# Token-tile order at the end of w_ff2 and w_down and at the start of the next projection, and VectorE's order at w_out and at the post-norms

## The chip, the cores and the metric
The kernel runs on one core of a Trainium2 chip, in one launch. The metric is the device time of that core in microseconds (us). TensorE (PE) multiplies, VectorE (DVE) and ScalarE (ACT) compute element by element, GpSimd (POOL) does small statistics and softmax scalings, and SyncE (SP) issues the transfers of the weights.

## The reference, cut to what matters
Four transformer layers run over 256 tokens of width 1024, all in fp32: two of a first kind, then two of a second.

```python
# first kind, x2
h = modulate(rmsnorm(x, norm1_g[l]), shift1, scale1)
proj = h @ w_in[l]                      # 1024 x 7200, with the gates
merged = g_a*(o_mla @ w_o_mla[l]) + g_b*(o_sb @ w_o_sb[l]) + g_c*(o_mb @ w_o_moba[l])
x = x + gate1 * (merged @ w_out[l])
h = modulate(rmsnorm(x, norm2_g[l]), shift2, scale2)
x = x + gate2 * (square(relu(h @ w_ff1[l])) @ w_ff2[l])     # w_ff2: 4096 x 1024
# between the kinds: x = rmsnorm(x, final_norm_g)
# second kind, x2
mix = hybrid_mixer(rms_norm(x, attn_pre_norm[l]), ...)      # w_in_2, attention, w_out_2
x = x + rms_norm(mix, attn_post_norm[l])
u = conv_ffn(rms_norm(x, ffn_pre_norm[l]), ...)             # w_up, conv, silu, w_down: 2816 x 1024
x = x + rms_norm(u, ffn_post_norm[l])
```

## The kernel before, in words
The 256 tokens are two token tiles, t = 0 and 1, of 128 each. A product of two fp32 values is made of three fast matmuls: each operand is split in a high part (rounded) and a low part (what is left), and high*high, high*low and low*high are added in PSUM (`three`).

Weights come in pieces of 128 x 1024 values (512 KB; 464 or 474 KB for the projections). A unit is four pieces. SyncE loads the pieces in stream order into a ring of ten places (`RAW`); the load of a piece waits until PE has told that the piece ten places earlier is used (`piece_used`, in the order of the stream). ScalarE then writes the piece's high part (L1195) into a second ring of four places (`HIGH`), whose place is free when PE has used the piece four earlier; the first unit of each projection has its high parts in `spare` memory instead. VectorE then writes the low part over the piece (L1562, `split_quarter`). Each engine works through its instructions strictly in the order in which the program has them. That order is written out by hand: `highs(n)` on ScalarE, `split_unit`, `first_quarters(n)` on VectorE.

`linear_deep` computes w_ff2 (8 units) and w_down (5 units of 4 pieces and one of 2). A piece here is 128 rows by all 1024 columns, and four PSUM banks collect t=0 (two halves of columns, i = 0 and 1) and t=1 (i = 2 and 3). Within a unit PE goes piece by piece over all four banks; in the last unit it goes bank by bank. The left operand is the hidden layer, split by VectorE unit by unit into two buffers used in turn (`split_hidden`, L1586 and L1587), in `split_unit(lambda j: hidden(g) if j == 0 else None)`, that is right behind the unit's first piece.

At the end of w_ff2 VectorE multiplies each bank by the gate row and adds it to x (`gated`, L1810 and L1812). ScalarE squares each part of x (L1214), GpSimd makes the reciprocal root (`rstd_parts`, L604), VectorE scales the tile (`scale_tokens`, L1555), PE turns it (`flip_tile`, eight transposes, L670), and both ScalarE and VectorE copy the turned tile out, in high and low parts (`features_out`, `split_tokens`, L1592 to L1596). Only then can the next projection start on this tile. Between the kinds of layer there is one more norm (`final_norm`, L1819). At the post-norms of the second kind the squares are of the banks, `normed` writes bank * rstd * row to `wide` (L1994) and adds it to x (L1997), and the same steps follow. GpSimd clears two buffers (L637, L638) at the start of each layer of the second kind, right behind the last root.

The first unit of a projection (`tokens_as_ready`) runs all of t=0, with the flips of t=1 behind its first quarter, then all of t=1. The units behind it run quarter by quarter over both tiles (`tokens_by_quarters`), and free a piece with each quarter. In layers of the first kind steps of the modulation (`ada_step`, two VectorE instructions on a piece of w_ada) are laid beside the units: `IN_STEPS` says how many pieces of w_ada follow each unit.

At w_out of the first kind `linear_pair` computes the third branch, (t=0: two units), (t=1: two units), with `flip_tile(merged, 0)` before the last. VectorE multiplies each bank by its gate (L1938), adds it to `wide` (L1940), and splits two pieces of w_out before the first of these four banks and two behind it.

Of the kernel before, what the change touches and what calls it, by code (L numbers as in the profile page):

```python
# [113 lines left out]
def two_blocks(nc, x_in, c_in, positions, w_ada, b_ada, norm1_g, norm2_g, w_in, q_norm_g, w_uq,  # L114
# [5 lines left out]
    with ctx:  # L120
# [3 lines left out]
        def sem(name):  # L124
# [11 lines left out]
            ("gates", [P, T, 3 * D]),  # L136
            ("ring", [P, RAW, PIECE]))
        with contextlib.ExitStack() as first:
            featT, oT, kvm, pT, sm, gates, ring = [first.enter_context(nc.sbuf_tensor(n, shape, F32)) for n, shape in shared]
        featT_r, oT_r, kvm_r, pT_r, sm_r, gates_r, ring_r = [sb(n + "_r", shape, F32R) for n, shape in shared]  # L140
# [4 lines left out]
        big = sb("big", [P, 33 * S])  # L145
# [19 lines left out]

        proj = big[:, 0:T * ATT].rearrange("p (t n) -> p t n", t=T)
# [25 lines left out]
        spare_1 = slots(kvm_r, 0, PIECE) + slots(sm_r, PIECE) + slots(pT_r, 0)  # L192
        spare_2 = slots(gates_r, 0, PIECE) + slots(sm_r, PIECE) + slots(pT_r, 0)
# [81 lines left out]
        gates_ready = sem("gates_ready")  # L275
        conv_done = sem("conv_done")
# [94 lines left out]
        IN_STEPS = [4, 4] + [2] * 8  # L371
        IN_OUT = {1: 4, 2: 5, 4: 6, 6: 7, 8: 8, 10: 9}
# [3 lines left out]
        for l in range(LAYERS1):  # L376
# [34 lines left out]
            for u in range(8):  # L411
                split(w_ff2[l], (0, D), rows=(4 * u, 4 * u + 4), per=1)
        for l in range(LAYERS2):
# [18 lines left out]
            for k0 in range(0, CH, 4):  # L432
                split(w_down[l], (0, D), rows=(k0, min(k0 + 4, CH)), per=1)
# [81 lines left out]
        def _(sp):  # L515
# [48 lines left out]
            for t in range(T):  # L564
                sp.wait_ge(part_ready, LAST_PART - 2 * (T - 1 - t))
                sp.dma_start(out[0][t * P:(t + 1) * P, :], x[:, t, :]).then_inc(out_stored, 16)
            sp.wait_ge(out_stored, 16 * T)
# [7 lines left out]
        def _(pool):  # L575
# [47 lines left out]
            TWICE = ((0, 0), (0, 1), (1, 0), (0, 0), (0, 1), (1, 1), (1, 0), (1, 1))  # L623
# [10 lines left out]
            rstd_parts(TWICE)  # L634
            for l in range(LAYERS2):
# [5 lines left out]
                rstd_parts(TWICE if l + 1 < LAYERS2 else IN_TURN)  # L641
# [3 lines left out]
        def _(pe):  # L645
# [130 lines left out]

            def gate_quarters():
# [82 lines left out]
            def linear_deep(chunks):  # L860
# [4 lines left out]
                for c0 in range(0, chunks, 4):  # L865
                    get, _n = next_quarters()
                    seen.more(hid_split)
                    k = min(4, chunks - c0)

                    last_unit = c0 + k == chunks  # L870
                    steps = [(i, kk) for i in range(4) for kk in range(k)] if last_unit else \
                        [(i, kk) for kk in range(k) for i in range(4)]
                    for i, kk in steps:
                        t, cols = i // 2, slice(i % 2 * 512, i % 2 * 512 + 512)
                        w = get(kk)
                        h = [hid_parts[:, c0 // 4 % 2, part, kk, t * P:(t + 1) * P] for part in range(2)]
                        last = c0 + kk == chunks - 1
                        three(open_[i][:, :], h, (w[0][:, 0, cols], w[1][:, 0, cols]), c0 + kk == 0, last,
                              owner[i].full if last else None)
                        if i == 3:  # L880
                            owed.append((piece_used, 1))
# [132 lines left out]
            for l in range(LAYERS1):  # L1014
# [7 lines left out]
                else:  # L1022
                    flip_tile(scaled, 0)
                    tokens_as_ready(scaled)
                for u in range(11):
                    if u == 0:
# [42 lines left out]
                linear_deep(FF1 // P)  # L1069

            for l in range(LAYERS2):
                flip_tile(scaled, 0)
                tokens_as_ready(scaled)
                in_2_tile0.append(made[id(for_act)])

# [1118 lines left out]
```

## Time and profile before

| | us |
|---|---|
| median of 3 runs | 1845.45 |
| lowest, highest | 1840.52, 1845.65 |
| the profiled execution | 1851.16 |
| its span, first to last instruction | 1849.4 |
| PE busy | 1724.8 (93%) |
| VectorE busy | 1180.2 (64%) |
| ScalarE busy | 836.0 (45%) |

The profile is of one execution. The granted TensorE clock was 0.971 of full on average over the span. Busy PE time includes matmuls at half clock, so 93% is not 93% of what the engine can do. A row of the waits says which engine's instruction at which line sat idle, for whom, how long in total, how often, and the longest. A row of the timeline has start, duration, engine, line, operation, output and inputs, count, and in square brackets the idle time before it with what ended it.

### The profile page before, as it was taken

To read this page: it belongs to the slowest core of one execution; us is meant where nothing else is said; L and a number is where in the kernel's file an instruction comes from. 1 tells how busy PE (TensorE), PEld (TensorE's weight loads), DVE (VectorE), ACT (ScalarE), POOL (GpSimd) and SP (SyncE) were. 2 spreads that over 40 slices of the span, in tenths; PEclk is the share of its full clock that TensorE was granted. 3 is DMA by queue.
4 is the path that set the end of the run, shared out by engine and by line. 5 is a ranking of instruction groups with operands and counts; after the bars stand their busy time and mean duration, and the time that the engine had idled before them with its cause. 6 is when DMAs were issued, how large, how long until landed. Compare 5 with 4: busy or idle time off the path is not lost. (4 is left out here: it accounts for less than half of the span.)

```text
span 1849.4 us, 25477 instructions
## 1 busy us (share of the span) xinstructions
PE 1724.8 (93%) x9675; PEld 1439.2 (78%) x9675; DVE 1180.2 (64%) x2144; ACT 836.0 (45%) x1467; POOL 127.9 (7%) x272
## 2 busy tenths in 40 slices
PE   7899999889999999998899989997999899979998
PEld 7787675579987886764799868755998687659996
DVE  3877555665667875556545675644778656537785
ACT  2345363245534442651455353453554444635553
POOL 1000111000000000210000010131000100410000
PEclk9999999989999999999899989898999999989999
DMA  9677424447765984336355537504655466036652
GB/s 330 256 263 243 137 92 159 160 143 255 263 192 162 338 269 140 114 105 214 129 188 194 193 119 215 161 1 137 183 183 185 147 194 182 1 114 183 183 186 86
DMA packets 185626, 323.75 MB, mean 175 GB/s; under 512 B 13508, under 2 KB 101152, under 8 KB 185504
## 3 DMA queue, kind: packets, MB, share of 16 engines
q1 hardware_dynamic: 182912, 320.54, 53.8%
q10 hardware_dynamic: 2592, 1.57, 0.3%
q8 instruction: 77, 1.26, 0.3%
q14 instruction: 45, 0.37, 0.1%
HBM read 321.02 MB, written 1.05 MB: 174 GB/s over the span
## 5 line engine op out<-in xcount | busy, mean ns | idle before, releaser
L1562 DVE TENSOR_TENSOR ring_r<-ring,high 128x1024 fp32r<-128x1024 f32 (+3 forms) x422 | 500.0, 1198 | 325.4 <-ACT high L1195 317.9
L1195 ACT ACTIVATE high<-ring 128x1024 fp32r<-128x1024 f32 (+3 forms) x422 | 435.1, 1039 | 552.4 <-PE bank L661 428.0
L661 PE MATMUL bank<-featT_r,high 128*128 128x256 f32 x1216 | 349.9, 288 | 17.6 <-DVE oT_r L1594 14.2
L661 PE MATMUL bank<-oT_r,high 128*128 128x256 f32 x1216 | 347.7, 286 | 0.0
L661 PE MATMUL bank<-featT_r,ring_r 128*128 128x256 f32 x1216 | 347.6, 286 | 0.0
L661 PE MATMUL bank<-ring_r,featT_r 128*128 128x464 f32 (+3 forms) x736 | 282.6, 384 | 0.0
L661 PE MATMUL bank<-high,gates_r 128*128 128x512 f32 x864 | 268.0, 390 | 2.2 <-DVE ring_r L1562 1.2
L661 PE MATMUL bank<-high,featT_r 128*128 128x512 f32 (+3 forms) x648 | 252.1, 389 | 9.3 <-DVE oT_r L1594 7.4
L661 PEld LDWEIGHTS bank<-featT_r,high 128*128 128x128 f32 x1216 | 237.3, 195 | 19.9 <-issue 16.0
L661 PE MATMUL bank<-high,oT_r 128*128 128x512 f32 (+3 forms) x648 | 246.6, 381 | 0.0
L661 PEld LDWEIGHTS bank<-oT_r,high 128*128 128x128 f32 x1216 | 237.4, 195 | 0.5 <-issue 0.5
L661 PEld LDWEIGHTS bank<-featT_r,ring_r 128*128 128x128 f32 x1216 | 237.1, 195 | 0.0
L661 PEld LDWEIGHTS bank<-high,gates_r 128*128 128x128 f32 x864 | 162.2, 188 | 37.6 <-DVE ring_r L1562 2.3
L661 PE MATMUL bank<-ring_r,gates_r 128*128 128x512 f32 x432 | 168.2, 389 | 0.0
L661 PEld LDWEIGHTS bank<-ring_r,featT_r 128*128 128x128 f32 x736 | 141.1, 192 | 21.1 <-issue 1.0
L661 PEld LDWEIGHTS bank<-high,featT_r 128*128 128x128 f32 x648 | 122.4, 189 | 33.6 <-issue 11.8
L661 PEld LDWEIGHTS bank<-high,oT_r 128*128 128x128 f32 x648 | 122.4, 189 | 18.8
L1642 DVE SCALAR_TENSOR_TENSOR ada<-ring,tiny,ada 128x512 f32<-128x512 f32 x154 | 115.4, 749 | 8.3 <-DMA ring<-in_w_ada 3.3
L611 POOL TENSOR_TENSOR sm<-sm,rs 128x128 f32<-128x128 f32 (+1 forms) x160 | 76.5, 510 | 389.5 <-DVEq L1738 389.5
L1276 ACT ACTIVATE sm<-sm,mx 128x128 f32<-128x128 f32 (+1 forms) x160 | 70.8, 443 | 57.3 <-DVE mx L1720 57.3
L661 PEld LDWEIGHTS bank<-ring_r,gates_r 128*128 128x128 f32 x432 | 81.1, 188 | 16.6
L600 POOL TENSOR_SCALAR stat<-stat 128x1 f32<-128x1 f32 x26 | 10.0, 386 | 981.0 <-ACT sm L1214 980.6
(242 smaller groups left out, 2002.2 us busy)
## 6 DMA issues: line engine op xcount, KB each, us to landing
ring<-in_w_ff SPq DMA_DIRECT2D x128, 512.0 KB, 4.4
ring<-in_w_ada SPq DMA_DIRECT2D x96, 512.0 KB, 5.3
ring<-in_w_up SPq DMA_DIRECT2D x176, 256.0 KB, 3.1
ring<-in_w_in SPq DMA_DIRECT2D x64, 464.0 KB, 5.4
ring<-in_w_in SPq DMA_DIRECT2D x48, 512.0 KB, 5.1
ring<-in_w_in SPq DMA_DIRECT2D x48, 474.0 KB, 4.2
ring<-in_w_down SPq DMA_DIRECT2D x44, 512.0 KB, 3.5
ring<-in_w_out SPq DMA_DIRECT2D x24, 512.0 KB, 5.3
```

The source lines that it names most:

```text
L600: pool.tensor_scalar(stat[:, 4 + t:5 + t], stat[:, 2 * t:2 * t + 1], EPS, None, ALU.add).then_inc(pool_chain, 1)
L611: ins = pool.tensor_tensor(sm[:, n, a:z], sm[:, n, a:z], rs[:, n, t:t + 1].to_broadcast([P, z - a]), ALU.mult)
L661: ins = pe.matmul(o, a, b, start=start, stop=stop, skip_group_check=True)
L1195: act.activation(it["high"], it["raw"], ACT.Copy).then_inc(high_ready, 1)
L1276: ins = act.activation(sm[:, n, cols], sm[:, n, cols], ACT.Exp, scale=jobs[i]["scale"], bias=mx[:, n, t:t + 1], accum_out=rs[:, n, t:t + 1])
L1562: dve.tensor_tensor(it["low"], it["raw"], it["high"].bitcast(F32), ALU.subtract).then_inc(low_ready, 1)
L1642: link(dve.scalar_tensor_tensor(out=acc, in0=row, scalar=by, in1=acc, op0=ALU.mult, op1=ALU.add))
```

## The change
`linear_deep` takes a list of unit sizes ([4]*8 for w_ff2, [4, 4, 4, 2, 4, 4] for w_down). Its last two units run by token tile: t=0 of the last but one, t=0 of the last, t=1 of the last but one, t=1 of the last. The turning of t=0 for the next projection is put inside the last unit's t=1 part. The last unit's high parts lie in spare memory (the buffer `big`). The next projection's first two units run t=0 of both, then t=1 of both, with the flips of t=1 inside the second. The modulation pieces beside these units move three units on. At w_out VectorE splits one piece behind each of the two t=0 banks and copies out the features of t=0 ahead of the last bank. At the post-norms the banks are multiplied by the row before the root is there, and one instruction multiplies by the root and adds to x. The result leaves in four transfers instead of two.

```diff
-        IN_STEPS = [4, 4] + [2] * 8
-        IN_OUT = {1: 4, 2: 5, 4: 6, 6: 7, 8: 8, 10: 9}
+        IN_STEPS = [0, 4, 4, 4] + [2] * 6
+        IN_OUT = {2: 4, 3: 5, 4: 6, 6: 7, 8: 8, 10: 9}
+        FF_UNITS, DOWN_UNITS = [4] * 8, [4, 4, 4, 2, 4, 4]
...
+            def two_as_ready(second, flip_at):
+                units = [next_quarters() for _ in range(2)]
+                for t, u, r in ((0, 0, for_dve), (0, 1, outputs), (1, 0, for_dve), (1, 1, for_dve)):
+                    ...
+                    for j in range(QUARTERS):
+                        if t == 0 and u == 1 and j == flip_at:
+                            flip_tile(second, 1)
...
             def linear_deep(sizes, ready=None, flip_at=0):
+                for u in range(tail):
+                    ...
+                for t in range(T):
+                    if t == 0:
+                        seen.more(hid_split)
+                    for kk in range(sizes[tail]):
+                        for i in (2 * t, 2 * t + 1):
+                            step(tail, i, kk)
+                    if t == 0:
+                        seen.more(hid_split)
+                    for i in (2 * t, 2 * t + 1):
+                        if ready is not None and i == 2 + flip_at:
+                            flip_tile(ready, 0)
+                        for kk in range(sizes[tail + 1]):
+                            step(tail + 1, i, kk)
...
+                    first_quarters(2)
+                    gated(l - 1, 1, 0, for_dve, 0, 0)
+                    gated(l - 1, 1, 1, for_dve, 0, 1)
+                    first_quarters(1)
                     scale_tokens([0])
+                    first_quarters(1)
+                    features_out(gain, shift, True, [0])
+                    gated(l - 1, 1, 2, outputs, 1, 0)
                     gated(l - 1, 1, 3, outputs, 1, 1)
+                    first_quarters(2)
                     scale_tokens([1])
+                    first_quarters(2)
+                    in_out(for_dve, 0, 0)
                     features_out(gain, shift, True, [1])
...
-                        if br == 2 and k == 5:
-                            first_quarters(2)
+                        if br == 2 and not t:
+                            first_quarters(1)
+                        if br == 2 and t and not hf:
+                            features_out(parts=True, tiles=[0])
-                features_out(parts=True)
+                features_out(parts=True, tiles=[1])
...
-                    split_unit(lambda j: hidden(g) if j == 0 else None)
+                    split_unit(lambda j: hidden(g) if j == (3 if g == 7 else 0) else None)
...
+            def products(g, t):
+                    dve.wait_ge(squares, next(squared))
+                    ins = dve.tensor_tensor(wide[:, t, cols], b[:, :], rowbc[:, g, cols], ALU.mult)
+            def normed(t):
+                seen.more(rstd_ready)
+                    dve.scalar_tensor_tensor(out=x[:, t, cols], in0=wide[:, t, cols], scalar=stat[:, 8 + t:9 + t],
+                                             in1=x[:, t, cols], op0=ALU.mult, op1=ALU.add).then_inc(part_ready, 1)
...
-                for g in range(1, (CH + 3) // 4):
-                    split_unit(lambda j: hidden(g) if j == 0 else None)
+                for g in range(1, len(DOWN_UNITS)):
+                    at = {4: 2, 5: 3}.get(g, 0)
+                    split_unit(lambda j: hidden(g) if j == at else None)
```

## Rows read from the trace of the kernel before

**Rows 1.** PE's waits over the whole span, the three largest.
```profile
PE bank L661 <- DVE oT_r L1594: 31.8, 9, 4.8
PE bank L670 <- DVE wide L1555: 30.3, 8, 7.1
PE bank L661 <- DVE ring_r L1562: 11.9, 9, 4.8
```

**Rows 2.** Busy time by stretch (stretch, length, PE PEld DVE ACT POOL, clock, DMA share, GB/s).
```profile
554.20:603.80 49.60, 45.76 (x209) 38.66 (x208) 37.87 (x52) 20.40 (x32) 3.46 (x6) 0.97 0.55 175
1068.90:1125.20 56.30, 47.84 (x208) 39.52 (x208) 37.75 (x48) 24.43 (x42) 8.23 (x14) 0.91 0.50 154
1444.90:1500.80 55.90, 47.27 (x209) 39.80 (x208) 35.24 (x46) 24.33 (x42) 6.81 (x14) 0.91 0.51 154
336.10:352.10 16.00, 10.02 (x30) 6.66 (x31) 7.28 (x11) 1.61 (x3) 0.00 (x0) 0.79 0.43 133
1820.00:1849.40 29.40, 21.82 (x97) 17.73 (x95) 14.32 (x17) 8.06 (x13) 1.96 (x6) 0.96 0.09 36
```

**Rows 3.** PE alone by stretch: w_ff2-like matmuls, projection matmuls.
```profile
1792.56:1841.82 49.26, 49.26 (x216) 1.00 0.30 97
588.26:603.38 15.12, 15.12 (x74) 1.00 0.78 261
```

**Rows 4.** PE alone by stretch, where the granted clock fell and did not.
```profile
338.40:341.80 3.40, 3.40 (x10) 0.50 0.50 146
580.80:584.10 3.30, 3.08 (x9) 0.50 0.37 141
1096.20:1106.30 10.10, 6.31 (x21) 0.50 0.17 50
704.30:727.00 22.70, 22.66 (x65) 1.00 0.54 171
```

**Rows 5.** Timeline of VectorE and PE at the first w_out.
```profile
334.55 2.36 DVE L1562 TENSOR_TENSOR ring_r<-ring,high 128x1024 fp32r<-128x1024 f32 x2
336.82 0.68 DVE L1938 TENSOR_TENSOR big<-bank,gates 128x512 f32<-128x512 f32 x1
344.67 0.69 DVE L1938 TENSOR_TENSOR big<-bank,gates 128x512 f32<-128x512 f32 x1 [4.87 <-PE bank L661]
338.39 1.94 PE L670 MATMUL bank<-cst,wide 128*128 128x128 f32 x8 [2.30 <-issue]
348.25 0.47 PE L661 MATMUL bank<-high,featT_r 128*128 128x512 f32 x1 [3.69 <-DVE oT_r L1594]
```

**Rows 6.** Timeline of ScalarE and VectorE in the last units of w_ff2.
```profile
1079.79 1.06 ACT L1195 ACTIVATE high<-ring 128x1024 fp32r<-128x1024 f32 x1 [1.66 <-PE bank L661]
1080.88 1.23 DVE L1562 TENSOR_TENSOR ring_r<-ring,high 128x1024 fp32r<-128x1024 f32 x1 [1.49 <-ACT high L1195]
1073.87 0.69 DVE L1586 CAST gates_r<-big 128x1024 fp32r<-128x1024 f32 x1
1074.59 1.22 DVE L1587 TENSOR_TENSOR gates_r<-big,gates_r 128x1024 fp32r<-128x1024 f32 x1
```

**Rows 7.** SyncE's weight loads issued from 571 to 579 us.
```profile
DMA to landing us min/median/max: 3.6/4.9/5.5
```

**Rows 8.** Timeline of VectorE around the root of t=0, behind w_ff2.
```profile
573.59 0.69 DVE L1812 TENSOR_TENSOR x<-x,wide 128x512 f32<-128x512 f32 x1
576.34 0.75 DVE L1555 TENSOR_SCALAR wide<-x,stat 128x1024 f32<-128x1024 f32 x1 [0.73 <-POOL stat L604]
```

**Rows 9.** The scaling's and GpSimd's clearing's lines (duration ns min/median/max, first and last start).
```profile
L1555 DVE TENSOR_SCALAR wide<-x,stat x16: 745/753/2409, 10.4 to 1647.8; 128x1024 f32<-128x1024 f32 x16
L638 POOL MEMSET kvm<- x2: 1799/1799/1799, 1100.8 to 1476.2; 128x2048 f32 x2
```

**Rows 10.** Timeline of VectorE at a post-norm, t=1 behind w_out_2.
```profile
1267.43 0.75 DVE L1994 SCALAR_TENSOR_TENSOR wide<-bank,stat,rowbc 128x512 f32<-128x512 f32 x1 [1.86 <-POOL stat L604]
1268.21 0.69 DVE L1997 TENSOR_TENSOR x<-x,wide 128x512 f32<-128x512 f32 x1
```

More of the change, by code:

```diff
@@ L411, in two_blocks @@
             for u in range(8):
-                split(w_ff2[l], (0, D), rows=(4 * u, 4 * u + 4), per=1)
+                split(w_ff2[l], (0, D), rows=(4 * u, 4 * u + 4), per=1, spare=spare_ff if u == 7 else None)
         for l in range(LAYERS2):
@@ L431, in two_blocks @@
                 split(w_up[l], (a0, a0 + 256), (b0, b0 + 256))
-            for k0 in range(0, CH, 4):
-                split(w_down[l], (0, D), rows=(k0, min(k0 + 4, CH)), per=1)
+            for u, k0 in enumerate(itertools.accumulate(DOWN_UNITS[:-1], initial=0)):
+                split(w_down[l], (0, D), rows=(k0, k0 + DOWN_UNITS[u]), per=1,
+                      spare=spare_down if u == len(DOWN_UNITS) - 1 else None)
         MLA_FILL, MOBA_FILL = {1: 4, 4: 4}, {1: 2, 3: 4}
@@ L563, in _ @@
                     broadcast_rows(attn_post[l], ffn_post[l])
[L564 to L567, printed above, removed]
+            for n in range(2 * T):
+                t, cols = n // 2, slice(n % 2 * 512, n % 2 * 512 + 512)
+                sp.wait_ge(part_ready, LAST_PART - (2 * T - 1 - n))
+                sp.dma_start(out[0][t * P:(t + 1) * P, cols], x[:, t, cols]).then_inc(out_stored, 16)
+            sp.wait_ge(out_stored, 16 * 2 * T)
         N_LATE = 16 * (8 * DEPTH + 2)
@@ L864, in linear_deep @@
                 open_ = [claim(r)[0] for r in owner]
-                for c0 in range(0, chunks, 4):
-                    get, _n = next_quarters()
-                    seen.more(hid_split)
[L868 to L881, printed above, removed]
+                gets = [next_quarters()[0] for _ in sizes]
@@ new lines, in linear_deep, with step @@
+                first = list(itertools.accumulate(sizes, initial=0))
+                chunks, tail = first[-1], len(sizes) - 2
+                def step(u, i, kk):
+                    t, cols = i // 2, slice(i % 2 * 512, i % 2 * 512 + 512)
+                    w = gets[u](kk)
+                    h = [hid_parts[:, u % 2, part, kk, t * P:(t + 1) * P] for part in range(2)]
+                    c = first[u] + kk
+                    three(open_[i][:, :], h, (w[0][:, 0, cols], w[1][:, 0, cols]), c == 0, c == chunks - 1,
+                          owner[i].full if c == chunks - 1 else None)
+                    if i == 3:
+                        owed.append((piece_used, 1))
@@ L1083, in blocks_turned @@
                                  outputs.full if a and t else None)
[L1085 removed]
+                for u in range(2, 6):
                     tokens_by_quarters((for_act, for_dve), blocks_turned if u == 4 else None)
@@ L1160, in _ @@
                     channels(for_dve, True)
-                linear_deep(CH)
+                linear_deep(DOWN_UNITS, scaled if l + 1 < LAYERS2 else None, 1)
         @block.scalar
@@ L2005, in stored_units @@
                     stored(for_dve)
-                    dve.wait_ge(for_act.read, in_2_tile0[l] + n - 1)
-                for u in range(6):
+                    dve.wait_ge(for_act.read, in_2_tile0[l] + n - 2)
+                in_2_out(outputs, 0, 1)
+                split_unit()
+                in_2_out(for_dve, 1, 0)
+                in_2_out(for_dve, 1, 1)
+                for u in range(2, 6):
                     if u == 4:
```

164 lines of the change are left out of this document (106 added, 58 removed).

## The prediction
> **What bounds the kernel now.** I read the waits of PE first, because PE is busy in nearly the whole span. Only three kinds are large: for the low features (31.8 us, 9 times), for the scaled token tile (30.3 us, 8 times), for a split weight piece (11.9 us) [rows 1]. The first two are the serial chain behind each linear layer: bank, gate or norm, squares, root, scale, flip, features. Then I cut the span into the stretches where the change works [rows 2]. There are seven: two w_out, two post-norms behind w_out_2, and the ends of w_ff2 and w_down: tail A (w_ff2 to the second w_in), tail B (w_ff2 to w_in_2), tail C (w_down to w_in_2), and the last w_down, behind which the kernel ends. The rows run from the start of the last eight pieces to the end of the projection's second unit: A 49.6, B 56.3, C 55.9 us; the last stretch to the end of the kernel is 29.4 us.
>
> The same matmuls without a wait: 216 in 49.26 us are 0.228 us each, so eight pieces (96 matmuls) take 21.9; projection matmuls are about 0.212 (15.12 us for 72 of them whole), two units 20.4, 20.8 with w_in_2's 474 columns [rows 3]. With two flips of 1.1 us an ideal tail is 44.4 (A) or 44.8. So A has only 5.2 us to give, B 11.5, C 11.1.
>
> Part of this is clock. Behind a wait of 2.30 us the granted clock was 0.50 for 3.4 us, behind one of 2.8 as well, behind a wait of 4.1 with another of 3.1 in it for 10.1; behind one of 1.6 it stayed 1.00 [rows 4]. Half clock is the 1.2 GHz level instead of 2.4: it costs half of what PE worked in the stretch, some 1.6 us for 3.4.
>
> **w_out (twice).** Now VectorE splits two pieces (2.36 us) between the first two banks, so the second product starts at 336.82, and PE's flip waits 2.30 us, to 338.39. After the change one piece lies there, 1.14 less: the flip starts near 337.25 behind a wait of 1.2 us. That is below the waits behind which the clock fell, so the flips and the last eight matmuls take 1.1 and 3.5 us instead of the 6.2 that they took at half clock: PE is through at 341.9, not 344.56. Meanwhile VectorE splits one piece (to 338.3), takes the third bank (to 339.7) and writes the features of t=0 (copy, cast and low part, 1.9 us, to 341.5). So t=0 can start at 341.9; before, the same copy stood behind the last bank's product at 344.67 and PE waited 3.69 us, to 348.25 [rows 5]. The flip of t=1 needs the last bank (product and add behind the features, to 343.5) and comes 0.3 us late. PE resumes behind the flips near 344.75 instead of 352.1. That is 7.4 us: 4.5 of waits and 2.9 of clock. If the clock falls anyway it is 4.5. Both layers have the same pattern: 7.4 x 2 = **14.8 gained** (9.0 to 14.8).
>
> **Post-norm behind w_out_2 (twice).** Behind the root VectorE had 0.78 + 0.61 twice, 2.86 us; now the product is made while GpSimd makes the root, and two instructions of 0.75 are left, 1.4 us less for the tile whose chain PE waits for [rows 10]. The clock stretch stays. **2.7 gained** (1 to 3).
>
> **The tails.** I take time 0 as PE's start of the last but one unit and follow each queue. Two things come late.
>
> First, the last hidden split. VectorE makes it behind all four pieces of the last unit (it was behind the first), so I count from the high ring. The last but one unit's fourth high part needs its place, which is free at time 0. From such a release the low part starts 1.1 us later; then five low parts of 1.15 each follow on VectorE (2.36 for two [rows 5]), then the cast and the split, 0.72 + 1.22 [rows 6]: 1.1 + 5.8 + 1.9 = 8.9 us with the semaphores. PE has done t=0 of the first of the two units at 5.45 and stands till 8.95: **3.5 us in A and B**, where before it had 0.6. In w_down the unit of two pieces puts the same problem one unit earlier: its second piece frees the high place at time 0, the hidden split of the next unit ends near 1.5, and the last one near 9.2, while PE is ready at 7.0: **1.5 + 2.2 us in C and at the end**. I expect 3.4 us at half clock behind the 3.5 and behind the 2.2, 1.6 us each; from both sides 0 to 5.
>
> Second, the ring of ten. Eight places hold the two last units, and none is released in their t=0 part, so the projection's third piece loads only when the first of t=1 is used: 14.4 + 1.4 + 0.35 = 16.1 (A, B), lands 3.6 later [rows 7], high part to 20.8, low part to 21.9. VectorE's list has this low part ahead of the scaling of t=0. The root is there earlier: 16.0 for the last gated part plus the 2.1 us from add to scaling [rows 8]. So the scaling ends at 22.7, while in A the flip stands before the last unit's t=1 part, at 19.85: a wait of **2.85 us**, again with half clock behind it (1.6). In B and C the flip stands 2.7 us later; B waits 0.7 there because final_norm comes in between, C nothing.
>
> Tile t=1. PE has t=0 of two units, 10.2 us, as cover for its chain. In A that is enough (scaling ready 5.3 us behind the last matmul, flip 6.4 behind it). In B the chain has final_norm, a second set of squares and a root; the second unit's first two pieces are split between these steps and come 0.7 and 1.2 us late, the flip 0.5, the features 1.4. On top comes GpSimd's clearing of 1.8 us, which starts with the root: the scaling that met it took 2.41 us instead of 0.75 [rows 9]. It does so again, 1.66 more. In C the product is already made; with the clearing the flip is 0.9 late and the features 1.5.
>
> On that clearing the Trainium skill (SBUF — State Buffer, Who interferes with whom) says that VectorE in a two-port mode and GpSimd share a port pair that one holds for the whole instruction. By that rule, the trace agrees (2.41 against 0.75 us), and the new order moves neither instruction away from the other; without the rule B and C would be 1.7 us better each.
>
> Sums, ideal plus the waits plus clock:
> - A: 44.4 + 3.5 + 1.6 + 2.85 + 1.6 = 54.0 against 49.6: **4.4 lost**.
> - B: 44.8 + 3.5 + 1.6 + 0.7 + (0.7 + 1.2 + 0.5 + 1.4 + 1.7) = 56.1 against 56.3: 0.2 gained.
> - C: 44.8 + 1.5 + 2.2 + 1.6 + 0.9 + 1.5 = 52.5 against 55.9: **3.4 gained**.
> - The end: PE's last eight pieces take 21.9 + 3.7 + 1.6; behind them two instructions of 0.75 instead of 2.86 us: 5.3 - 1.4 = **3.9 lost**. The last transfer is half as large; no row has one of that size, so I count nothing for it.
>
> **Modulation pieces.** Three units in a row now have a w_ada piece beside each weight piece. VectorE needs 1.15 + 1.6 us for such a pair, four pairs and copies 12.0 us a unit, PE 10.2 to 11.2; it had a lead for two units, and in the third PE waits some 0.8 us, per layer: **1.5 lost** (0 to 3). The first layer's start loses nothing else, and its second unit's weights arrive earlier.
>
> **Sum.** -14.8 - 2.7 + 4.4 - 0.2 - 3.4 + 3.9 + 1.5 = -11.3 us. On the profiled execution's 1851.2 (span 1849.4 and 1.8 around it) that is 1839.9. That execution was 5.7 above the median of the runs, so on the median: 1845.45 - 11.3, about **1834**. A measurement of this kernel can tell 0.3%, 5.5 us, from no change.
>
> **The rivals.**
> - *The last hidden split is not late* (ScalarE or VectorE reach it in time, or PE has slack that I don't see). The tails lose 3.5 + 1.6 twice and 3.7 + 1.6 twice less: 20.8 more gained, 1813. For it: VectorE waits 1.2 to 1.5 us ahead of each low part [rows 6], so it has room. Against it: the wait there is for the high part, whose place PE itself frees, and the split stands last in the list. 0.13.
> - *The clock stays at half for 10 us behind each tail's wait*, as it did in B before. The place is the t=0 part of the last unit and the flip in A, five waits of over 2 us; each costs (10.1 - 3.4) / 2 = 3.4 more, 17 us in all: 1851, slower. It decides from three such waits on (1844 to 1848). For it: 10.1 us behind 4.1 [rows 4]. Against it: that stretch had a second wait of 3.1 in it, which kept PE idle; in the tails dense matmuls follow. 0.13.
>   The Trainium skill (TensorE: Matmul & The Clock Gate, What's actually happening) has the low clock as the state that an idle engine falls to and steady work releases. By that rule, the trace agrees with both lengths, and the dense matmuls behind the new waits speak for the short one.
> - *w_out's gain is handed back at the next weights*: w_ff1's pieces come no earlier because the loads are the limit. Then 14.8 goes and the total is +3.5: 1849, within 0.3%. For it: PE waited for a split piece nine times. Against it: around w_out the DMA share was 0.43 [rows 2]; these loads start when PE releases places, and so move with it. 0.14.
>
> **How the numbers follow.** The forecast (1826 to 1840) has 0.60, the rivals 0.13, 0.13 and 0.14. Faster by over 0.3% is the forecast less its upper rim, and the first rival: 0.70. Within 0.3%: the third rival, part of the second and the forecast's rim, 0.18. Slower: 0.12. The range 1820 to 1847 leaves out most of the first rival and the worse half of the second.
>
> **What would show it.** In the changed trace PE should stand about 3.5 us for the hidden split (line of L1587) in both w_ff2 tails and 1.5 and 2.2 in both w_down; a flip in A should wait for the scaling some 2.9 us, with a low part of the third projection piece just ahead of it on VectorE; at w_out the wait for the low features should be gone and the flip's about 1.2; at the post-norms 7.1 should be 5.7. If the hidden split's wait is missing, the forecast is too slow by up to 20 us; if the clock stretches behind these waits are 10 us long, too fast by up to 17.

## The result: slower, by 0.4 to 0.8%

| | changed | before |
|---|---|---|
| median, first comparison | 1858.28 us (4 runs, 1857.50 to 1860.21) | 1845.55 us |
| ratio, 95% interval | 1.0077 [1.0058, 1.0096] | |
| median, second comparison | 1857.44 us (10 runs, 1847.07 to 1859.16) | 1849.09 us |
| ratio, 95% interval | 1.0037 [1.0019, 1.0055] | |
| profiled span | 1858.5 us | 1849.4 us |

The forecast was 1834. The two intervals do not overlap, so executions of one kernel vary by more than either says. Some of this variation lies ahead of all the work that was changed: the first matmul of the first projection starts between 45.4 and 49.9 us, from one profiled execution to another, in kernels that do not differ there. Whether that explains the two medians is not shown. So below, the stretches are compared inside the profiles, and the totals only where they differ by more.

Where PE waits in the changed kernel (the view of the waits, whole span; it answers to [rows 1], with lines moved: L676 flips, L667 is a matmul, L1605 scales, L1637 is the hidden split, L1644 the low features, L1612 the low weight part).

```profile
PE bank L676 <- DVE wide L1605: 36.6, 9, 6.4
PE bank L667 <- DVE gates_r L1637: 18.9, 8, 3.6
PE bank L667 <- DVE oT_r L1644: 16.1, 5, 5.7
PE bank L667 <- DVE ring_r L1612: 9.8, 10, 4.8
```

The waits for the features halved, as meant. The waits for the scaled tile did not fall but rose by 6.3 us (30.3 to 36.6), though w_out's and the post-norms' part of them fell, and the hidden split is a new row of 18.9.

The four tails, from the start of the last eight pieces (in w_down with the wait of 1.78 just ahead of them) to the end of the projection's second unit or of the kernel. Columns as in [rows 2].

```profile
543.00:601.00 58.00, 48.56 (x210) 41.02 (x210) 32.56 (x46) 21.61 (x34) 2.35 (x6) 0.91 0.37 115
1060.40:1124.40 64.00, 51.20 (x210) 41.98 (x209) 36.46 (x48) 24.37 (x42) 7.23 (x14) 0.87 0.34 105
1443.30:1502.80 59.50, 48.67 (x210) 39.90 (x210) 35.46 (x46) 23.89 (x42) 7.07 (x14) 0.94 0.37 112
1822.20:1858.50 36.30, 25.31 (x97) 19.96 (x96) 14.95 (x17) 7.60 (x13) 1.96 (x6) 0.88 0.08 29
```

| us | A | B | C | end |
|---|---|---|---|---|
| before | 49.6 | 56.3 | 55.9 | 29.4 |
| forecast | 54.0 | 56.1 | 52.5 | 33.3 |
| measured | 58.0 | 64.0 | 59.5 | 36.3 |
| missed by | 4.0 | 7.9 | 7.0 | 3.0 |
| measured again (experiment 7) | 58.1 | 61.6 | 56.6 | 36.2 |

The four misses are 21.9 us. Between the same two profiles the whole was missed by 20.4 (9.1 longer, where 11.3 shorter was forecast), between the first medians by 24. The last row is a second profile of the same changed kernel: its tails add up to 212.5 us, where the first has 217.8, so a tail varies by up to 3 us from one execution to the next. The waits in these stretches, from the timeline of PE, in the order A (two rows), B (three), C (three) and the end, whose first wait of 1.78 is C's again:

```profile
552.25 0.50 PE L667 MATMUL bank<-big_r,gates_r 128*128 128x512 f32 x1 [3.60 <-DVE gates_r L1637]
570.86 1.97 PE L676 MATMUL bank<-cst,wide 128*128 128x128 f32 x8 [5.84 <-DVE wide L1605]
1069.57 0.79 PE L667 MATMUL bank<-big_r,gates_r 128*128 128x512 f32 x1 [3.60 <-DVE gates_r L1637]
1092.39 1.97 PE L676 MATMUL bank<-cst,wide 128*128 128x128 f32 x8 [6.39 <-DVE wide L1605]
1108.73 1.66 PE L676 MATMUL bank<-cst,wide 128*128 128x128 f32 x8 [1.95 <-DVE wide L1605]
1445.09 0.50 PE L667 MATMUL bank<-high,gates_r 128*128 128x512 f32 x1 [1.78 <-DVE gates_r L1637]
1454.41 0.79 PE L667 MATMUL bank<-big_r,gates_r 128*128 128x512 f32 x1 [3.58 <-DVE gates_r L1637]
1472.97 1.09 PE L676 MATMUL bank<-cst,wide 128*128 128x128 f32 x8 [3.33 <-DVE wide L1605]
...
1833.36 0.79 PE L667 MATMUL bank<-big_r,gates_r 128*128 128x512 f32 x1 [3.58 <-DVE gates_r L1637]
```

The hidden split's 3.5 (A, B) and 1.5 are there nearly as forecast (3.60 and 1.78). Not as forecast: the flip of t=0 waits 5.84, 6.39 and 3.33 us, where 2.85, 0.7 and 0 stood, and the second hidden wait of w_down is 3.58 instead of 2.2. The clock goes with them. PE alone (length, busy, granted clock, DMA share, GB/s), behind A's two waits, B's first two and the end's second:

```profile
552.75:556.10 3.35, 3.35 (x10) 0.50 0.00 0
570.90:576.60 5.70, 5.70 (x18) 0.50 0.31 85
1069.70:1074.90 5.20, 5.20 (x13) 0.50 0.00 0
1092.50:1095.40 2.90, 2.90 (x11) 0.50 0.00 0
1833.50:1839.50 6.00, 6.00 (x15) 0.50 0.00 0
```

### The profile page after: what moved, and what is told of

Its sections match the earlier page's. It is cut to its first block and busy times, and to the rows that moved or that the text cites. A ratio compares the mean times of both kernels' runs of the same rounds, so it can differ in the third digit from the quotient of the medians.

```text
span 1858.5 us, 25496 instructions
## 1 busy us (share of the span) xinstructions
PE 1730.6 (93%) x9675; PEld 1442.8 (78%) x9675; DVE 1182.0 (64%) x2147; ACT 833.4 (45%) x1464; POOL 124.6 (7%) x272
## 5 line engine op out<-in xcount | busy, mean ns | idle before, releaser
L1612 DVE TENSOR_TENSOR ring_r<-ring,high 128x1024 fp32r<-128x1024 f32 (+3 forms) x406 | 480.5, 1198 | 316.4 <-ACT high L1233 307.7
L1233 ACT ACTIVATE high<-ring 128x1024 fp32r<-128x1024 f32 (+3 forms) x406 | 418.4, 1038 | 524.4 <-PE bank L667 415.0
L667 PE MATMUL bank<-featT_r,high 128*128 128x256 f32 x1216 | 350.0, 288 | 16.6 <-DVE oT_r L1644 15.0
L667 PE MATMUL bank<-oT_r,high 128*128 128x256 f32 x1216 | 347.9, 286 | 0.0
L667 PE MATMUL bank<-featT_r,ring_r 128*128 128x256 f32 x1216 | 347.7, 286 | 0.0
L667 PE MATMUL bank<-ring_r,featT_r 128*128 128x464 f32 (+3 forms) x736 | 280.5, 381 | 0.0
L667 PE MATMUL bank<-high,featT_r 128*128 128x512 f32 (+3 forms) x648 | 252.0, 389 | 3.6 <-DVE ring_r L1612 3.1
L667 PEld LDWEIGHTS bank<-featT_r,high 128*128 128x128 f32 x1216 | 237.4, 195 | 18.9 <-issue 16.8
L667 PE MATMUL bank<-high,oT_r 128*128 128x512 f32 (+3 forms) x648 | 246.4, 380 | 0.0
L667 PEld LDWEIGHTS bank<-oT_r,high 128*128 128x128 f32 x1216 | 237.4, 195 | 0.5 <-issue 0.5
L667 PEld LDWEIGHTS bank<-featT_r,ring_r 128*128 128x128 f32 x1216 | 237.3, 195 | 0.0
L667 PE MATMUL bank<-high,gates_r 128*128 128x512 f32 x736 | 229.3, 390 | 4.6 <-DVE gates_r L1637 4.6
L667 PE MATMUL bank<-ring_r,gates_r 128*128 128x512 f32 x432 | 173.0, 400 | 0.0
L667 PEld LDWEIGHTS bank<-high,gates_r 128*128 128x128 f32 x736 | 138.2, 188 | 34.9 <-DVE gates_r L1637 6.2
L667 PEld LDWEIGHTS bank<-ring_r,featT_r 128*128 128x128 f32 x736 | 139.8, 190 | 20.7 <-issue 0.7
L667 PEld LDWEIGHTS bank<-high,featT_r 128*128 128x128 f32 x648 | 122.5, 189 | 28.8 <-issue 6.8
L667 PEld LDWEIGHTS bank<-high,oT_r 128*128 128x128 f32 x648 | 122.4, 189 | 18.5
L667 PEld LDWEIGHTS bank<-ring_r,gates_r 128*128 128x128 f32 x432 | 84.4, 195 | 17.6
```

Source lines behind the costliest of these rows:

```text
L667: ins = pe.matmul(o, a, b, start=start, stop=stop, skip_group_check=True)
L1233: act.activation(it["high"], it["raw"], ACT.Copy).then_inc(high_ready, 1)
L1612: dve.tensor_tensor(it["low"], it["raw"], it["high"].bitcast(F32), ALU.subtract).then_inc(low_ready, 1)
```

## Why the flip waits: one blocked instruction ahead of the chain

Rows of the timeline of ScalarE and VectorE in A, from the last hidden split to the scaling of t=0:

```profile
550.98 1.22 DVE L1637 TENSOR_TENSOR gates_r<-big,gates_r 128x1024 fp32r<-128x1024 f32 x1
561.21 0.98 ACT L1233 ACTIVATE kvm_r<-ring 128x928 fp32r<-128x928 f32 x1 [12.88 <-PE bank L667]
562.22 1.13 DVE L1612 TENSOR_TENSOR ring_r<-ring,kvm_r 128x928 fp32r<-128x928 f32 x1 [10.02 <-ACT kvm_r L1233]
564.63 0.68 DVE L1860 TENSOR_TENSOR wide<-bank,rowbc 128x512 f32<-128x512 f32 x1
569.02 1.13 DVE L1612 TENSOR_TENSOR ring_r<-ring,sm_r 128x928 fp32r<-128x928 f32 x1 [1.65 <-ACT sm_r L1233]
570.06 0.75 DVE L1605 TENSOR_SCALAR wide<-x,stat 128x1024 f32<-128x1024 f32 x1
```

VectorE stood idle for 10 us while the banks of t=0 came full. The next thing in its list was the low part of the projection's first piece. That waits for ScalarE's high part. The description of the kernel before says only that this one goes to spare memory, but it waits too, until PE has used the piece eight before it among the split pieces. In the old order of units that piece was used in time; in A of the kernel before, ScalarE made the first two of these high parts with no idle time in front:

```profile
566.14 1.83 ACT L1195 ACTIVATE kvm_r<-ring 128x928 fp32r<-128x928 f32 x2
```

Now it is the first of the last but one unit, which PE frees only in the t=1 part, near 561 us here. Gating (L1860) is behind it in VectorE's list and starts at 564.63. I call this theory Q (the queue). My forecast had only the ring of ten and the *third* piece; theory R is that this alone makes the wait. Theory H is that the late hidden split is a second loss, in series with the first.

## The experiments

Ratios are to the kernel before, with the 95% interval. The changed kernel itself stands at 1.0077 and 1.0037.

**1. The two small edits alone**, on the kernel before: VectorE's order at w_out, and the product ahead of the root at the post-norms (both as in the diff of the change).

> The kernel before with only the edits at w_out and at the post-norms; the tails as they were, the output in two transfers. Every theory that puts the loss in the tails expects the forecast's 14.8 + 2.7 here, about 17 us faster than before (1828, or 1825 if the 3 us that the changed kernel also gained between w_out and the tail come with it), with the flip's wait at w_out 1.2 us and the wait for w_out's features gone. A rival that has w_out's gain handed back at the next weights expects 1845. If it is 1828, the tails of the changed kernel cost some 30 us, not 10.

Measured: 1832.65 us, 0.9907 [0.9888, 0.9927]. So these edits gain some 17 us, as forecast (17.5), and the loss lies in what this kernel leaves out: the tails, the modulation's move and the output in four transfers. The changed kernel is 1.3 to 1.7% above this one, where I had reckoned 6.2 us (0.3%).

**2. w_out alone**, on the kernel before:

```diff
-                        if br == 2 and k == 5:
-                            first_quarters(2)
+                        if br == 2 and not t:
+                            first_quarters(1)
+                        if br == 2 and t and not hf:
+                            features_out(parts=True, tiles=[0])
...
-                features_out(parts=True)
+                features_out(parts=True, tiles=[1])
```

> The kernel before with only VectorE's new order at w_out. 14.8 to 16.5 us below the kernel before (0.8 to 0.9%), 1.2 us flip wait at each w_out, and the post-norms' waits of 7.1 us as before; the version with the post-norm edit too is 2.7 us below it. A rival that gives the post-norm edit more than that (its products also free the banks earlier) expects less than 13 here.

Measured: 1835.15 us, 0.9929 [0.9904, 0.9953], 13 us. The rival in which w_out's gain is handed back at the next weights falls; it expected about the kernel before. The post-norms' 2.7 us is about what lies between 1 and 2, inside their intervals.

**3. The high parts' wait taken away** from the first unit of each projection w_in and w_in_2 (`free` is set for these alone; their places are spare memory), order kept:

```diff
-                    before, own = split_pieces[q - 8] if q >= 8 else None, spare
+                    before, own = split_pieces[q - 8] if q >= 8 and not free else None, spare
```

> The changed kernel, where the high parts of the next projection's first unit no longer wait for the piece eight back (their spare memory has been free for long). Theory Q, the queue: t=0's gating stands on VectorE behind the low parts of that unit's first two pieces, whose high parts wait until PE is in the t=1 part. Then the first gating starts as soon as the bank is full, about 4 us earlier, and what is left is the wait for the third piece, whose load needs a place of the ring of ten: flip waits of 2.9 (A), 0.7 (B) and about 0 (C) instead of 5.8, 6.4 and 3.3; 9 to 12 us faster than the changed kernel, about 1848. Rival R, the ring of ten alone (the third piece's load sets the flip now too): the flip waits stay as they are, 1858.

Measured: 1840.74 us, 0.9953 [0.9937, 0.9969]. The first gating in A now starts when its bank is full, 6.8 us behind the hidden split (552.80 and 546.00, starts) where it was 13.7 (564.63 and 550.98), and only the third piece stands ahead of the scaling:

```profile
552.80 0.69 DVE L1860 TENSOR_TENSOR wide<-bank,rowbc 128x512 f32<-128x512 f32 x1 [3.51 <-PE bank L667]
...
558.32 0.57 POOL L611 TENSOR_TENSOR stat<-stat,half 128x1 f32<-128x1 f32 x1
561.09 0.98 ACT L1233 ACTIVATE sm_r<-ring 128x928 fp32r<-128x928 f32 x1 [3.13 <-DMA ring<-in_w_in]
562.10 1.12 DVE L1612 TENSOR_TENSOR ring_r<-ring,sm_r 128x928 fp32r<-128x928 f32 x1 [4.89 <-ACT sm_r L1233]
563.14 0.75 DVE L1605 TENSOR_SCALAR wide<-x,stat 128x1024 f32<-128x1024 f32 x1
563.95 1.97 PE L676 MATMUL bank<-cst,wide 128*128 128x128 f32 x8 [2.75 <-DVE wide L1605]
```

This is the forecast's picture for A, 2.75 us where it said 2.85. So R is real and is that large in A; the rest of the 5.84 was Q. In B and C the flip of t=0 does not wait at all, so there the whole wait was Q. The root was there at 558.9, and the scaling stood 4.2 us behind a piece that a transfer held. The four tails add up to 202.3 us, 15.5 less than in the first profile of the changed kernel and 10.2 less than in the second. The total is 17 us below the changed kernel, where 9 to 12 was expected; part of the excess may be the program's start, 4.4 us earlier in this profile (45.5) than in the changed kernel's first (49.9). The same holds for the totals of experiments 4 to 6, whose profiles start at 45.4 to 45.8.

**4. The chain of t=0 ahead of all four pieces**, on VectorE and ScalarE, waits kept. Shown is VectorE at the second w_in; its other two places and ScalarE's `highs` are moved in the same way:

```diff
-                    first_quarters(2)
                     gated(l - 1, 1, 0, for_dve, 0, 0)
                     gated(l - 1, 1, 1, for_dve, 0, 1)
-                    first_quarters(1)
                     scale_tokens([0])
-                    first_quarters(1)
+                    first_quarters(4)
...
```

> The changed kernel with gating, norm and scaling of t=0 ahead of all four split pieces of the next projection, on VectorE and ScalarE. Theory Q expects all three flip waits gone (0 to 0.5) and the clock stretch behind them too: 15.5 us of waits and 3 to 6 of clock, some 18 us faster than the changed kernel, about 1840, if four split pieces behind the scaling (4.6 us) are done before the last bank is (5.4 us in B and C's case 2.7, where up to 2 us can come back as a wait for features). Rival H, the hidden splits set the tails: the flip waits move into other waits and the time stays within 3 us of 1858.

Measured: 1835.23 us, 0.9929 [0.9909, 0.9949]. The flip of t=0 waits no more (in A it runs at full clock with no idle time before it); what is left of PE's waits:

```profile
PE bank L676 <- DVE wide L1602: 21.1, 7, 5.7
...
PE bank L667 <- DVE gates_r L1634: 17.3, 8, 3.6
```

36.6 became 21.1; the hidden split's row stands (18.9 before, and 1.6 of the difference is C's second wait, see experiment 10). The features of t=0 are 1.93 us late in B, because the pieces that were moved behind the scaling lie before the copies.

**5. The hidden split early**: w_ff2's last one right behind its unit's first piece, w_down's behind the second piece of one unit and the first of the other.

```diff
-                    split_unit(lambda j: hidden(g) if j == (3 if g == 7 else 0) else None)
+                    split_unit(lambda j: hidden(g) if j == 0 else None)
...
-                    at = {4: 2, 5: 3}.get(g, 0)
+                    at = {4: 1}.get(g, 0)
```

> The changed kernel with the last hidden split behind the last unit's first piece instead of its fourth, and w_down's last but one behind the second piece. The split then ends 5.4 us behind the start of the tail, just when PE wants it, and the last pieces' low parts come 1.3 us late instead: waits for the hidden split 3.6 to about 0 and 1.8 to 0, waits for a low part 0 to 1.3. In A and B the flip does not move earlier by the same, since the chain ahead of it hangs on PE's t=1 part, which moves with it. Theory H expects 2 x (3.6 - 1.3) + 2 x (5.4 - 1.3) = 12.8 of waits and 1.6 of clock at four places, up to 19 us faster than the changed kernel, about 1842. Theory Q alone, with the hidden splits hidden behind something, expects 1858.

Measured: 1836.27 us, 0.9933 [0.9910, 0.9956]. The waits of 3.6 and 1.8 for it are gone and the scaled tile's row stays to the tenth; the row of the low weight parts rises from 9.8 to 11.8 us:

```profile
PE bank L676 <- DVE wide L1605: 36.6, 9, 6.4
```

**6. Both, 4 and 5.**

> The changed kernel with both edits: the chain of t=0 ahead of the split pieces, and the hidden splits early. Theory Q+H (two separate waits in series, one ahead of the last unit's t=0 part, one ahead of the flip): the gains add, 18 to 23 us and 16 to 19 us, 35 to 40 us below the changed kernel and 1 to 1.3% below the kernel before; waits in the tails: hidden split 0, low parts 1.3 spread, flips of t=0 none. Rival (one wait hides the other; whichever is removed first gives all): no more than the better one of the two, about 1.4% below the changed kernel.

Measured: 1820.02 us, 0.9853 [0.9828, 0.9877]. The four tails, as above:

```profile
537.50:585.10 47.60, 45.73 (x211) 37.32 (x210) 32.53 (x46) 21.93 (x34) 2.63 (x6) 1.00 0.45 140
1044.20:1098.30 54.10, 49.38 (x210) 39.90 (x209) 36.40 (x49) 24.03 (x42) 6.89 (x14) 0.94 0.42 126
1416.70:1466.50 49.80, 46.59 (x211) 37.44 (x210) 34.05 (x45) 23.89 (x42) 6.88 (x14) 1.00 0.44 135
1785.00:1814.50 29.50, 23.17 (x97) 17.54 (x96) 13.55 (x16) 7.60 (x13) 1.96 (x6) 0.97 0.09 36
```

Against the changed kernel's 217.8 us in all, experiment 4 has 199.6, experiment 5 has 197.4, and this one 181.0. The parts, 18.2 and 20.4, add to 38.6, and both together give 36.8. Against the changed kernel's second profile (212.5) it is 12.9 and 15.1, and 31.5 for both. By either, both together give far more than the better one alone, and experiment 4 left the hidden waits of A and B as they were, experiment 5 the flips' waits. So Q and H are two waits in series, and neither hides the other; how exactly they add is not settled by single profiles. The clock is 1.00 in A and C: the half-clock stretches were a share of both losses.

**7. The changed kernel again**, beside these.

> The changed kernel itself, so that the others can be compared with it on one chip. Before and changed differ by 0.8% again; the waits in the four tails are those of its first profile within 0.1 us (3.6 and 5.8, 3.6 and 6.4, 1.8 and 3.6 and 3.3, 1.8 and 3.6). If the difference to the kernel before is only in the start of the program (before w_in's first unit, which came 1.2 us later in the changed profile and 3 to 4 us earlier in those of the last three experiments), it is not the change's, and the ratio is nearer to 1.

Measured: 1857.44 us, 1.0037 [1.0019, 1.0055]. All waits of t=0's flip came back to 0.1 us; in C the second hidden wait was 1.97 here, at the end 3.58 again. The ratio was not 0.8% again, though the profile's start (48.9) is near that of the kernel before (48.7); the profiled execution, 1851.48, is one of the shorter of the ten.

**8. Both, and early high parts** (edits 3 and 5; two pieces ahead of the chain of t=0, two behind its scaling).

> The changed kernel with early hidden splits, with high parts of the next projection's first unit that wait for nothing, its first two pieces split ahead of t=0's chain and the other two behind the scaling. Theory Q+H: VectorE splits the two pieces while it would wait for the bank, so two pieces fewer (2.3 us) stand between the scaling and the features, and the wait for features that chaining ahead left in B (1.9 us) and C (0.5) goes: 2 to 4 us below the version with both edits. If that version's features were not what PE waited for, the same time.

Measured: 1818.07 us, 0.9840 [0.9816, 0.9865]; not to be told from 6. The wait for features went as expected, from 1.92 to 0.51 us in B and from 0.63 to none in C, but in B two waits for low parts (0.68 and 0.76) came up. B was left with this, timeline of VectorE, GpSimd and PE at the root of t=1:

```profile
1078.62 2.41 DVE L1605 TENSOR_SCALAR wide<-x,stat 128x1024 f32<-128x1024 f32 x1 [1.10 <-POOL stat L611]
1078.68 1.81 POOL L644 MEMSET kvm<- 128x2048 f32 x1
1081.09 1.09 PE L676 MATMUL bank<-cst,wide 128*128 128x128 f32 x8 [1.96 <-DVE wide L1605]
```

**9. GpSimd's clearing moved** to where the attention's input is there, on 8:

```diff
-                pool.wait_ge(part_ready, x1 + PARTS2 * l)
+                pool.wait_ge(nsa_in, l + 1)
```

> The best version so far (x7: the changed kernel with the hidden split early, the spare high places filled at once and the gating and scaling of t=0 ahead of the last two split pieces), with one edit: GpSimd's clearing of the attention sums (1.8 us) no longer starts with the root of t=1 in the tails behind w_ff2 and w_down, but only once the attention's input is there. If the clearing is what makes VectorE's scaling of t=1 slow (2.41 us where other executions of it take 0.75), the scaling takes 0.75 in B and C, PE's wait for the scaled tile of t=1 in B goes from 1.96 to some 0.3, in C the waits 0.80 and 1.09 (scaled tile, low features) go to near 0, and the kernel is some 3.5 us (0.2%) under x7's 1818.07, about 1814 to 1816. If the 2.41 has another cause, the same waits stand and the time is x7's. If the later clearing itself is late for the attention, PE waits there and the time is above x7's by up to 1.8 us a layer.
> On this the Trainium skill (SBUF — State Buffer, Who interferes with whom) says that a tensor_scalar of VectorE in a two-port mode and an instruction of GpSimd hold one shared pair of ports in turn, each for the whole instruction; by that rule the scaling is quick as soon as nothing of GpSimd lies beside it.

Measured: 1815.04 us, 0.9828 [0.9811, 0.9844]. The same place:

```profile
1083.16 0.75 DVE L1605 TENSOR_SCALAR wide<-x,stat 128x1024 f32<-128x1024 f32 x1 [1.10 <-POOL stat L611]
1083.97 1.09 PE L676 MATMUL bank<-cst,wide 128*128 128x128 f32 x8 [0.31 <-DVE wide L1605]
```

The scaling took 0.75 us in both layers, the flip's wait fell from 1.96 to 0.31, and C's from 0.79 to none, as expected; its wait for features went from 1.09 only to 0.65, and in B one of 1.08 came up behind. B and C became 2.1 and 1.5 us shorter. The gain of 3 us in the medians agrees, though the intervals of 8 and 9 overlap.

On this the Trainium skill (SBUF — State Buffer, Who interferes with whom) says that the shared ports go to whoever issues first, for its whole instruction, and the other is blocked. The trace agrees that one is blocked: 2.41 us beside the clearing, ending 0.54 behind it, and 0.75 us apart from it. It does not show that the first to issue gets the ports: by the recorded starts the scaling was first by 0.06 us, and it was the one that was held.

**10. A free piece told promptly**, on the changed kernel: the piece's own last matmul tells it, not the next matmul.

```diff
+                elif frees:
+                    ins.then_inc(piece_used, 1)
...
-                    if i == 3:
+                    if i == 3 and last:
```

> The changed kernel with one edit: a weight piece that PE has read is told as free by its own last matmul, where before the news rode on the matmul behind it (which at a bank's edge is one that may itself wait). Theory: w_down's unit of two pieces frees the second place only when PE resumes behind the first late hidden split, which makes the second hidden wait 3.6 us in C and at the end where 2.2 was forecast. With prompt news the second wait is some 1.9 to 2.2 in both, the hidden waits of A and B stay 3.6, their flip waits stay 5.8 and 6.4, and the kernel is 3 to 5 us faster than the changed one (1853 to 1856 beside 1857.4 to 1858.3). Rival: the second wait comes from VectorE's load alone (four pieces and the split of a unit against PE's pace); then it stays at 3.6 and the time is the changed kernel's.

Measured: 1849.73 us (12 runs), 1.0008 [0.9997, 1.0019], so 8 us under the changed kernel by the medians, 0.3 to 0.7% by the ratios. The edit tells every piece of w_ff2 and w_down promptly, not only those of the unit of two. The second hidden wait is 1.81 in C and 1.80 at the end, here the end of the changed kernel, then of this one (ScalarE's high part and PE's wait):

```profile
1824.58 1.06 ACT L1233 ACTIVATE high<-ring 128x1024 fp32r<-128x1024 f32 x1 [3.71 <-PE bank L667]
```
```profile
1819.23 1.06 ACT L1237 ACTIVATE high<-ring 128x1024 fp32r<-128x1024 f32 x1 [1.66 <-PE bank L667]
1828.29 0.50 PE L667 MATMUL bank<-big_r,gates_r 128*128 128x512 f32 x1 [1.80 <-DVE gates_r L1641]
```

In the changed kernel the news that the unit's second piece is free rode on the first matmul *behind* the wait of 1.78, so one wait made the next. That C's second wait was 1.97 in experiment 7 without this edit has another cause: there the clock fell behind the wait of 1.78, PE worked at half clock for 3.4 us, some 1.7 us longer for the same work, and so came that much later to the second wait. In the first profile, and at the end in both, it did not fall there and the wait was 3.58. PE alone behind C's first wait in experiment 7, and its second wait:

```profile
1441.60:1444.90 3.30, 3.30 (x9) 0.50 0.53 147
1449.93 0.50 PE L667 MATMUL bank<-big_r,gates_r 128*128 128x512 f32 x1 [1.97 <-DVE gates_r L1637]
```

The end is 4.6 us shorter (29.8 from its first matmul, after 34.4): 1.8 of wait, and the rest the clock, which fell behind 3.58 and not behind this 1.80. C is 1.9 us shorter than in the changed kernel's first profile; beside its second (a wait of 1.97 already) it is no shorter. The other hidden waits and the flip waits of A, B and C became shorter by 0.23 us each, one matmul. Expected were 3 to 5 us in all, and the end's 4.6 with C's 0 to 1.9 is near that. What the remaining microseconds of the 8 are is not shown; the two profiled executions do not differ by them (1852.28 here, 1851.48 in experiment 7).

**11. All**: 8, 9 and 10.

> x7 with both edits: the clearing behind the attention's input and the prompt news of a free weight piece. If the clearing is the cause of the slow scaling, 3.5 us under x7; the prompt news has little left to give here, because x7 waits for no hidden split: 0 to 2 us more. So 1812 to 1816. If neither bears, 1818, as x7.

Measured: 1811.37 us, 0.9810 [0.9795, 0.9825], the fastest of all, 46 to 47 us under the changed kernel. B, the worst tail, at full clock:

```profile
1043.50:1093.90 50.40, 47.03 (x210) 37.27 (x210) 34.70 (x48) 24.25 (x42) 4.99 (x12) 1.00 0.43 134
```

## Why the prediction was wrong, step by step

- **w_out: right.** Forecast 7.4 us twice; the timeline that answers to [rows 5]:

```profile
337.01 1.06 PE L676 MATMUL bank<-cst,wide 128*128 128x128 f32 x8 [1.17 <-issue]
341.61 0.47 PE L667 MATMUL bank<-high,featT_r 128*128 128x512 f32 x1
343.50 1.09 PE L676 MATMUL bank<-cst,wide 128*128 128x128 f32 x8 [0.27 <-DVEq L2014]
344.35 0.48 PE L667 MATMUL bank<-high,featT_r 128*128 128x512 f32 x1
337.10:352.10 15.00, 14.63 (x64) 1.00 0.45 138
```

  The flip's wait is 1.17 (1.2 said), the wait for the features is gone, t=1's flip is 0.27 late (0.3), and PE resumes at 344.35 (344.75), at full clock (last row, PE alone). Experiment 2 has 13 us by the ratio, 14 by the medians, of 14.8.
- **Post-norms: right.** The wait of 7.1 is 5.7, and one pair of instructions is left behind the root:

```profile
1266.80 1.41 DVE L2086 SCALAR_TENSOR_TENSOR x<-wide,stat,x 128x512 f32<-128x512 f32 x2 [0.26 <-POOL stat L611]
1270.73 1.97 PE L676 MATMUL bank<-cst,wide 128*128 128x128 f32 x8 [5.71 <-DVE wide L1605]
```

- **The last hidden split: right in A and B** (3.60 for 3.5) and in w_down's first (1.78 for 1.5). The rival that it is not late falls.
- **The wait of the flip of t=0: this step failed.** The prediction named two things that come late, and for the flip only the ring of ten: the projection's third piece, with "this low part ahead of the scaling". Of the steps ahead of it, it said "The root is there earlier: 16.0 for the last gated part". That is what was wrong. The gating itself stands behind the low parts of the first two pieces, and I left out the wait of their high parts on ScalarE, for the piece eight back. The last gated part came 24.4 us behind the start of A, not 16.0. The ring's part was right: measured alone it is 2.75 us (experiment 3). With the missing wait the gating starts 6.9 us later, and the flip waits 5.84 instead of 2.85 in A, 6.39 instead of 0.7 in B, 3.33 instead of 0 in C: 12.0 us of waits. With this one wait taken away (experiment 3) the tails are 202.3 us, where 195.9 were forecast and 217.8 measured.
- **The second wait in w_down: mis-sized.** 2.2 was for a piece freed when PE has done it; the news came with the next matmul, behind a wait. 3.58 measured where the clock did not fall between the two waits, 1.80 with prompt news.
- **The clock: the short stretch was the forecast, and it was too cheap.** I had 1.6 us once or twice a tail. PE worked at 0.50 for 3.35 and 5.7 us in A, 5.2 and 2.9 (and a third of about 3.4) in B, 6.0 at the end; half of each is the cost: A 4.5 instead of 3.2, B 5.8 instead of 1.6, the end 3.0 instead of 1.6, and C 3.1 instead of 1.6 (2.8 and 3.4 us). That is 8.4 us, over a third of the miss. In the tails no stretch was 10 us, so the rival as priced did not come, but half of its 17 us did. The rows read for this were too few: between w_out and w_ff1 PE of the kernel before worked at half clock for 5.5 us, behind a wait of 4.4 (from 384.08). In the second profile the clock did not fall behind B's hidden wait (3.60) nor behind C's flip (3.32), which makes much of the difference between the two profiles' tails.
- **t=1, the clearing:** 2.41 us again in B and C, and its cost is shown by experiment 9. B's late pieces and flip (0.76 and 1.95 us) were half of the 5.5 forecast; in C 2.15 came for 2.4.
- **The output:** 5.6 us lie behind the last matmul, 7.6 before; 1.4 forecast for the instructions and none for the transfer. With whole transfers it was 6.3 (experiment 1), so the halves give 0.7.
- **Modulation:** three waits of 0.29, 0.41 and 0.48 us in the second layer's w_in, 1.2 where 0.8 stood; in the first layer's nothing of the kind. So 1.2 for 1.5.
- **A small slip:** 15.12 us for 72 matmuls are 0.210 each, not 0.212; the ideal tails come out 0.2 us too long by it.

Together: 12.0 us of flip waits, 2 × 1.7 of w_down's hidden waits, 0.2 of w_ff2's and 8.4 of clock, less 2.8 in B and 0.3 in C for t=1 and 0.6 for the output. That is 20.3 of the 21.9 missed in these two profiles; the rest is not placed.

## What to carry to other kernels

When PE's order of reading changes, list for every instruction that stands ahead of the critical chain, on every engine, *all* the places it waits for, also those that cost nothing before; the ring that one looks at is not the only one. Put the chain's steps ahead of prefetched work that waits for something PE does only later, or take the wait away where it protects nothing. And see on which instruction a release rides: if it is the next one, a wait there delays the release too.

## What the runs showed of the hardware that was not expected

- In the tails of the changed kernel's first profile, waits on PE of 3.3 to 6.4 us were each followed by half-clock work of 2.8 to 6.0 us. Behind waits of 1.8 to 2.0 us a stretch of 3.4 us was there in C of experiment 10 and in B, and not at the end of experiment 10. In the second profile none came behind waits of 3.60 (B) and 3.32 (C). So the same wait in the same place can cost 1.4 to 3 us more or not. Two waits in series, with 12.8 us of work between them in A, each got a stretch of its own.
- VectorE's scaling of 0.75 us became 2.41 when a clearing of 1.8 us on GpSimd started 0.06 us behind it, in all 20 such meetings of the thirteen profiles; in two others the clearing had begun 0.72 us ahead (0.73 in one) and the scaling took 1.62. Moved apart (experiments 9 and 11), never.
- The first projection's first matmul fell in two groups, with the same work ahead of it: at 45.4 to 45.9 us in seven profiles and at 48.7 to 49.9 in six. In the seven the granted clock was 0.50 from about 24 to 51 us, in the six it was 1.00 there. The early start goes with the *lower* clock; why is not shown. The 4.5 us between the extremes are more than several of the effects studied here. A comparison of totals at 0.3% needs many runs, or stretches.
